# One order for early and middle expert rows: ScalarE casts their weights, VectorE gates middle rows in place, and their u tiles are asked for sooner

## The reference, cut to what matters

```python
q = xn @ wq                        # 8 heads x 2 halves x 128
top 16 of 128 keys for each half, then top 16 of their pair sums per head
gates = softmax(the 16 pair sums); expert = key_i * 128 + key_j
h = gelu(xn . peer_u[expert])      # 8 x 16 experts for each token
out = sum over those experts of gates * h * peer_v[expert]
```

## Time and profile before

| what | value |
|---|---|
| median of 3 runs | 3246.3 us (3240.91 to 3247.57) |
| the profiled execution's own time | 3233.7 us |
| span of its instructions | 3231.9 us |
| TensorE busy | 3097.7 us, 96% |
| VectorE busy | 2371.6 us, 73% |
| ScalarE busy | 1403.3 us, 43% |
| DMA over the span | 199 GB/s |
| mean granted TensorE clock | 0.977 |

### The profile page before, as it was taken

How to read it: one execution, slowest core, us unless ns; L and a number is a source line. 1 busy time by engine, 2 the same in 40 slices (tenths; PEclk the granted TensorE clock), 3 DMA queues, 4 the chain that set the end, 5 groups by cost and what they waited for, 6 DMA issues and landing times. The chain is left out here.

```text
span 3231.9 us, 52114 instructions
## 1 busy us (share of the span) xinstructions
PE 3097.7 (96%) x17744; PEld 2679.3 (83%) x17744; DVE 2371.6 (73%) x4997; ACT 1403.3 (43%) x2729; POOL 632.0 (20%) x556
## 2 busy tenths in 40 slices
PE   7899999999999999899999999999999998999999
PEld 5767776777867999888987799999789986899998
DVE  5667776776666677565978788788656887887887
ACT  5454333332336665475356333333465274333332
POOL 0000000000000000064434132222356061222221
PEclk9999999999999999899999999999999999999999
DMA  6115533434322545433545799999434518899996
GB/s 222 43 59 183 176 144 113 154 124 158 110 71 87 174 156 168 148 121 115 170 130 210 274 354 356 328 356 356 159 101 140 183 50 318 313 353 339 343 357 249
DMA packets 176414, 643.50 MB, mean 199 GB/s; under 512 B 20352, under 2 KB 20736, under 8 KB 175360
## 3 DMA queue, kind: packets, MB, share of 16 engines
q1 hardware_dynamic: 138672, 504.62, 45.0%
q0 software_dynamic: 36864, 134.23, 11.3%
q10 hardware_dynamic: 720, 2.71, 0.2%
HBM read 640.44 MB, written 1.05 MB: 198 GB/s over the span
## 5 line engine op out<-in xcount | busy, mean ns | idle before, releaser
L338 ACT ACTIVATE split<-ring 128x512 fp32r<-128x512 f32 (+1 forms) x644 | 397.6, 624 | 699.4 <-PE ps L224 666.5
L224 PE MATMUL ps<-hT,split 128*128 128x512 f32 (+1 forms) x3504 | 631.1, 341 | 6.5 <-DVEq L322 3.4
L224 PEld LDWEIGHTS ps<-hT,split 128*128 128x128 f32 x3504 | 546.5, 191 | 91.3 <-DVE hT L593 9.7
L347 POOL TENSOR_TENSOR split<-ring,split 128x512 fp32r<-128x512 f32 x184 | 244.3, 1338 | 1528.3 <-ACT split L338 1523.7
L2718 PE MATMUL ps<-h2F,gates 128*128 128x192 f32 x3008 | 519.2, 326 | 0.0
L347 DVE TENSOR_TENSOR split<-ring,split 128x512 fp32r<-128x512 f32 (+1 forms) x460 | 307.2, 678 | 283.3 <-ACT split L338 282.4
L2718 PEld LDWEIGHTS ps<-h2F,gates 128*128 128x128 f32 x3008 | 498.4, 190 | 17.1
L2784 ACT ACTIVATE split<-ring 128x512 fp32r<-128x512 f32 x504 | 317.4, 632 | 358.3 <-PE ps L2735 333.6
L2844 DVE TENSOR_TENSOR split<-ring,split 128x512 fp32r<-128x512 f32 x504 | 340.1, 689 | 118.0 <-ACT split L2784 115.4
L2708 POOL DMA_INDIRECT gates<-peer_rows,row_at x256 | 267.7, 1046 | 809.9 <-DVE row_act L2851 462.9
L2731 PE MATMUL ps<-split,chunk 128*128 128x512 f32 x512 | 232.1, 453 | 16.9 <-DVE chunk L2815 16.3
(11 more groups left out here) (394 smaller groups left out, 4758.2 us busy)
## 6 DMA issues: line engine op xcount, KB each, us to landing
ring<-peer_v SPq DMA_DIRECT2D x256, 512.0 KB
gates<-peer_u SPq DMA_DIRECT2D x200, 512.0 KB, 6.9
ring<-w_up SPq DMA_DIRECT2D x88, 512.0 KB, 3.8
ring<-w_choose SPq DMA_DIRECT2D x88, 512.0 KB, 3.5
ring<-w_mixing SPq DMA_DIRECT2D x68, 512.0 KB, 3.6
ring<-w_merge SPq DMA_DIRECT2D x64, 512.0 KB, 4.1
ring<-w_down SPq DMA_DIRECT2D x44, 512.0 KB, 3.7
mix_row_ring<-w_mod SPq DMA_DIRECT2D x40, 512.0 KB, 3.7
```

What stands on the lines that cost most here:

```text
L224: ins = nc.tensor.matmul(out, lhsT(a), rhs(b), start=first and n == 0, stop=last and n == len(PASSES) - 1)
L338: self.nc.scalar.activation(self.split[:, self.half_slot(s), 0, cols], self.ring[:, self.slot(s), cols], ACT.Copy).then_inc(self.high_read ...
L347: (ops or self.nc.vector).tensor_tensor(self.split[:, self.half_slot(s), 1, cols], self.ring[:, self.slot(s), cols], self.split[:, self.ha ...
```

## The change

In `experts_stage` the 34 early and middle rows now form one uniform list in `order`. Their weights are cast by ScalarE between the two halves of `high(j)`, and VectorE makes their lows between the two halves of `low(j)`. The middle rows are gated in place by VectorE at steps 1, 5, 9, 13, 17 and 21. `weigh` is left for late rows. In `choose_stage` the six middle u tiles are asked for among the last w_choose tiles. In `first_block` one sum of the modulation goes from place 5 to place 9.

```diff
-            up_sums = [(2, merge_rows[3]), (5, out_rows[0]), *(...)]
+            up_sums = [(2, merge_rows[3]), (9, out_rows[0]), *(...)]
 choose_stage, SyncE:
             for t in range(RAW, n_tiles):
                 slot_free(t - RAW)
                 weights.fetch(sp, t // RAW, t % RAW)
+                if 0 <= t - HC - RAW < MID:
+                    q = t - HC - RAW
+                    sp.dma_start(k.row_ring[:, q, :], tile(k.peer_u, l * (NK - EARLY) + q)).then_inc(k.mid_in, 16)
             for s in range(SPLIT):
                 slot_free(n_tiles - RAW + s)
                 ahead.fetch(sp, 0, s)
             ahead.begun = SPLIT
-            for q in range(MID):
-                sp.dma_start(k.row_ring[:, q, :], tile(k.peer_u, l * (NK - EARLY) + q)).then_inc(k.mid_in, 16)
 experts_stage:
-    order = [*((True, j) for j in range(EARLY)), (False, 0), (False, 1),
-             *(x for r in range(rows - 2) for x in ((True, EARLY + r), (False, r + 2))), (True, NK - 2), (True, NK - 1)]
+    given = EARLY + MID
+    order = [*((True, j) for j in range(given - 2)),
+             *(x for q in range(MID, rows) for x in ((True, EARLY + q - 2), (False, q))), (True, NK - 2), (True, NK - 1)]
+    given_of = lambda j: one(k.early, j) if j < EARLY else k.mid[(j - EARLY) // 2][:, (j - EARLY) % 2, :]
-    places = sorted([*range(3, EARLY, 4), *(t for t in range(EARLY + 2 * MID, len(order)) if is_v[t]), *range(EARLY + 2 * MID + 1, len(order) - 8, 6)])
+    places = sorted([*range(3, given, 4), *(t for t in range(given, len(order)) if is_v[t]), *range(given + 3, len(order) - 8, 6)])
 ScalarE:
+            def given_high(j):
+                if j >= EARLY:
+                    act.wait_ge(mid_gated, j - EARLY + 1)
+                act.wait_ge(halves_used, (j + SPLIT) * 2 - 2)
+                nc.scalar.activation(k.weight[:, j % 2, 0:DENSE], given_of(j), ACT.Copy).then_inc(weight_step, 1)
             def high(j):
                 act.wait_ge(weights.loaded[j % RAW], 16 * (j // RAW + 1))
                 for half, cols in enumerate(weights.halves):
+                    if half and j < given:
+                        given_high(j)
...
+            for j in range(SPLIT):
+                given_high(j)
...
-                if not v and n >= MID:
+                if not v:
                     activate(n)
 VectorE:
-            def split_early(j):
-                w, high = one(k.early, j), k.weight[:, j % 2, 0:DENSE]
-                dve.wait_ge(halves_used, (j + SPLIT) * 2 - 2)
-                nc.vector.tensor_copy(high, w).then_inc(weight_step, 1)
+            def split_given(j):
                 dve.wait_ge(weight_step, j + 1)
-                lows(w, j % 2)
+                lows(given_of(j), j % 2)
+            def gate_mid(q):
+                nc.vector.tensor_tensor(given_of(EARLY + q), given_of(EARLY + q), dense[:, :, q], ALU.mult).then_inc(mid_gated, 1)
             def weigh(q):
...
-                if q >= MID:
-                    dve.wait_ge(gelu_done, q - MID + 3)
+                dve.wait_ge(gelu_done, q - MID + 3)
...
             def low(j):
                 for half, cols in enumerate(weights.halves):
+                    if half and j < given:
+                        split_given(j)
...
-                if t + SPLIT < EARLY:
-                    split_early(t + SPLIT)
                 if not v:
                     weigh(n)
+                if t % RAW == 1 and t // RAW < MID:
+                    gate_mid(t // RAW)
```

More of the change, by code:

```diff
@@ L1567, in first_block @@
             up_places = [4 + 3 * t // 2 for t in range(3 * DC)]
-            up_sums = [(2, merge_rows[3]), (5, out_rows[0]), *((up_places[(n + 1) * DC - 1] + 2, p) for n, p in enumerate(up_rows))]
+            up_sums = [(2, merge_rows[3]), (9, out_rows[0]), *((up_places[(n + 1) * DC - 1] + 2, p) for n, p in enumerate(up_rows))]
             ffn_up_stage(k, w_up, tokens, w_down, ffn_norm, ModRows(k, up_rows, up_places, up_sums) if first else None)
@@ L2660, in experts_stage @@
     rows_there = lambda n: 16 * (l * len(range(n % ROW_SLOTS, 2 * sums, ROW_SLOTS)) + n // ROW_SLOTS + 1)
-    with stage(nc, *WEIGHT_SEMS, "u_in_0", "u_in_1", "u_in_2", "u_in_3", "u_done", "gelu_done", "weight_step", "weighted", "kept_0", "kept_1", "turned", "added", "stored", "ahead_high", "ahead_low",
+    with stage(nc, *WEIGHT_SEMS, "u_in_0", "u_in_1", "u_in_2", "u_in_3", "u_done", "gelu_done", "mid_gated", "weight_step", "weighted", "kept_0", "kept_1", "turned", "added", "stored", "ahead_high", "ahead_low",
                "row_step", "row_gelu", "row_weighed", *Norm.SUMS, weights=weights) as (
-            block, high_ready, low_ready, halves_used, u_in_0, u_in_1, u_in_2, u_in_3, u_done, gelu_done, weight_step, weighted, kept_0, kept_1, turned, added, stored, ahead_high, ahead_low,
+            block, high_ready, low_ready, halves_used, u_in_0, u_in_1, u_in_2, u_in_3, u_done, gelu_done, mid_gated, weight_step, weighted, kept_0, kept_1, turned, added, stored, ahead_high, ahead_low,
             row_step, row_gelu, row_weighed, squared, sums_done):
@@ L2816, in lows @@
                 ins.then_inc(weighted, 1)
-            def split_early(j):
-                w, high = one(k.early, j), k.weight[:, j % 2, 0:DENSE]
-                dve.wait_ge(halves_used, (j + SPLIT) * 2 - 2)
-                nc.vector.tensor_copy(high, w).then_inc(weight_step, 1)
+            def split_given(j):
                 dve.wait_ge(weight_step, j + 1)
-                lows(w, j % 2)
+                lows(given_of(j), j % 2)
+            def gate_mid(q):
+                nc.vector.tensor_tensor(given_of(EARLY + q), given_of(EARLY + q), dense[:, :, q], ALU.mult).then_inc(mid_gated, 1)
             def weigh(q):
                 j, buf = q + EARLY, q % 2
-                high, active = k.weight[:, buf, 0:DENSE], k.mid[q // 2][:, q % 2, :] if q < MID else k.gelu[:, buf, 0:DENSE]
-                if q >= MID:
-                    dve.wait_ge(gelu_done, q - MID + 3)
+                high = k.weight[:, buf, 0:DENSE]
+                dve.wait_ge(gelu_done, q - MID + 3)
                 dve.wait_ge(weighted, j + 2)
                 dve.wait_ge(halves_used, v_used(j - 2))
-                nc.vector.tensor_tensor(k.gated[:, 0:DENSE], active, dense[:, :, q], ALU.mult).then_inc(weight_step, 1)
-                dve.wait_ge(weight_step, j * 2 - EARLY + 1)
+                nc.vector.tensor_tensor(k.gated[:, 0:DENSE], k.gelu[:, buf, 0:DENSE], dense[:, :, q], ALU.mult).then_inc(weight_step, 1)
+                dve.wait_ge(weight_step, j * 2 - given + 1)
                 nc.vector.tensor_copy(high, k.gated[:, 0:DENSE]).then_inc(weight_step, 1)
-                dve.wait_ge(weight_step, j * 2 - EARLY + 2)
+                dve.wait_ge(weight_step, j * 2 - given + 2)
                 lows(k.gated, buf)
@@ L2866, in _ @@
             for j in range(SPLIT):
-                split_early(j)
+                split_given(j)
             for t, (v, n) in enumerate(order):
```

## The result

The changed kernel takes 3217.1 us (median of 10 runs, 3208.7 to 3238.8) against 3255.0 us of the kernel before (median of 10 runs, 3240.9 to 3262.7): a ratio of 0.9908, with a 95% interval of 0.9883 to 0.9932. That is 0.92% or some 30 us less by the ratio (22 to 38 us by its interval), and 28.7 us less was forecast; the two medians lie further apart, 37.9 us. The ten times of the changed kernel fall in two groups, seven from 3208.7 to 3222.6 us and three from 3234.5 to 3238.8 us, so a median depends on which group has more of them.

What follows compares the result with a forecast made beforehand. TensorE, busy 96%, bounds the kernel; only its waits and low clock before the late rows can be won. 2 x (3.4 + 6.65 + 1.3 - 0.6 - 0.1) = 21.3, plus 0.9 and 6.5: 28.7 off 3246.3 gives 3217.6 us, range 3208 to 3232.

Steps and rivals of the forecast that it cites:

- Middle rows: Combines 27 to 32: without gating, cast and lows right ahead of TensorE, no gap or half clock; 6.65 us less per layer.
- Combines 10 to 27: Early expert rows: moving the cast off VectorE gives it room, so combines run at 2.34 us; 3.4 us less per layer.
- The cast on ScalarE: 128x192 weight copy between both halves of `high`: 0.36 us, hidden; 0.1 us more per layer at the stage's start.
- The start: Combines 0 to 10, DMA bound: 1.3 us of 3.7 won per layer, less 0.6 for sooner gathers and 0.1 for the cast.
- Rival B: DMA sets the whole early part, gathers holding back v tiles beyond tile 10; early part wins nothing, 3225.8 us; chance 0.10.
- The u tiles: Scatter start: asking sooner for the middle u tiles makes layer 1 like layer 2; 0.9 us less.
- Place 9: Up stage: sum moved from place 5 avoids the bias-step wait and lost clock; 6.8 less 0.3 for later copy, 6.5 us less.
- Rival A: Early part still set by VectorE or ScalarE's hand-over; combines 10 to 27 keep 43.2 us, 3224.4 us; chance 0.11.
- Rival C: Middle stall moves to the first late rows, whose weights come late; 13.3 us lost, 3230.9 us; chance 0.05.
- D: Late rows start from full DMA queues and take 5.12 us each; 37.6 us more, 3255 us; chance 0.04.
- Rival E: Something unseen hides a stall, the change does little: within 6.5 us of the old time; chance 0.04.
- The signs: Expected in the profile: combines 2.34 us apart from 10 to 32, no gap above 0.3; wrong if ScalarE awaits v tiles after tile 10.

Runs made afterwards that it cites:

- run 4: Kernel before, early rows only: cast on ScalarE, weights between the halves; middle rows as before. Combines 27 to 32 take 18.10 and 18.34 us, 10 to 27 39.76 and 39.77.
- run 3: Changed kernel with the casts back on VectorE, same new order; in layer 2 combines 10 to 27 take 39.77 us and 27 to 32 11.67 us.
- run 1: Changed kernel without the sooner u tiles and with the sum back at place 5: 3229.1 us, ratio 0.9934 to the kernel before.
- run 9: The changed kernel unaltered, measured again in a second series on another chip: 3233.3 us, ratio 0.9916 to the kernel before.
- run 5: Kernel before with only the early weights' place moved between VectorE's two v tile lows, cast still on VectorE: combines 10 to 27 take 39.75 and 39.92 us.
- Run 6: Kernel before with only the early casts moved to ScalarE, weights' lows still after both v tile lows: combines 10 to 27 take 42.09 and 41.40 us.
- run 11: Changed kernel with only gathers 2 to 11 held back for the early rows in front: first ten combines 23.4 us, 32 combines 74.8 us, in both layers.
- Run 7: Kernel before with only the middle u tiles asked for sooner: VectorE's scatter start to combine 0 takes 69.3 us in layer 1, 67.9 in layer 2.

## Why the prediction was right, and where it was not

The saving was right: 28.7 us forecast, 27.9 us measured in the traces at the places aimed at (29.0 us without the scatter stretches), 29.9 us by the ratio (3255.0 x 0.0092). That the time itself came out at 3217.1 us for a forecast of 3217.6 us is luck: the base of 3246.3 us was 8.7 us under the median of ten runs, the medians then differed by 37.9 us, 9.2 us more than forecast, and the two cancel. The same kernel's second series had its median at 3233.3 us, just outside the range of 3208 to 3232 us. By its own terms:

- **Middle rows**, 6.65 us a layer: 7.15 and 6.68 us measured. The mechanism stands by run 4 (the stall stays without the new order) and run 3 (it goes with it, wherever the cast is done); which part of the new order does it stays open.
- **Combines 10 to 27**, 3.4 us a layer: 2.9 and 3.0 us measured, and 3.4 us in runs 1, 3, 4 and 9 (39.8 us). What is left in the profiled execution is the one combine that waits for its v tile. Here the size was about right and the step was wrong. "Four steps and a dot are 9.3 us of the 9.36 us that four combines take: no room for its waits" was the reason given, and the cast's way to ScalarE was to be the cure. Run 3 makes the cast on VectorE and loses nothing; run 5 moves only the weights' place in VectorE's queue and gains all. The step that failed is this sum: it was 0.6 us too large in four combines, and it missed that the last thing done in a step was the first thing wanted. Run 6 shows what moving the cast is worth by itself: 1.1 and 1.8 us of the 3.4.
- **The cast on ScalarE**, taken as 0.36 us and hidden: 0.36 us measured (mean of 64), and hidden. It is not needed for combines 10 to 32 (run 3).
- **The start**, 1.3 less 0.6 less 0.1 = 0.6 us a layer: 1.0 and 1.3 us measured. The 0.6 us taken off for the dot that asks sooner for the next gather was too much here, but the stretch itself varies: run 1 has 0.4 us less than before in layer 1 and 1.5 us in layer 2. That DMA keeps most of the 3.7 us held for this change: TensorE waits there for lows whose tiles landed late. It is no limit of the stage: with the gathers held back all of it can be had (run 11). The 411 GB/s "in its first 20 us" is a window of 6 us; over combines 0 to 10 it was 399 and 390 GB/s, at a share of 1.00.
- **Rival B** was right in its mechanism and wrong in its reach. In the row at the start of this stage the DMA engines move 402 GB/s at a share of 1.01, and with fewer gathers ahead the v tiles are in time (run 11). The rule of the Trainium skill (DMA: Bandwidth & Descriptors, Queues, rings and completion order), turns between the queues that have work, agrees with the even shares of the two queues there, 51.1% to 50.9% and 50.0% to 51.8%. But the gathers cost 2.1 and 2.4 us in combines 0 to 10 and 0.6 us in 10 to 27 (0.1 us in runs 1, 3 and 9), not the 3.4 us of the rival. That fits the 1.7 us of slack that the prediction gave a low in the steady part.
- **The u tiles**, 0.9 us: nothing. "With the tiles there early, layer 1 becomes like layer 2" failed: the row showed a wait of TensorE, and the step took the 0.9 us between two stretches for its price. Run 7 takes the wait away and leaves the stretch; what looked like a difference of layers is within the spread of a stretch of 67.9 to 69.8 us. The fetches ahead of it lose nothing in the changed kernel, as costed (from place 16 to the scatter it is 1.3 us longer, in a stretch of 1075 us, which takes 1071 to 1077 us over the fourteen traces).
- **Place 9**, 6.5 us: 6.9 us in the trace. The 0.3 us for the later copy was not needed.
- **Rival A** (the hand-over still paces): no. Combines run 2.34 us apart with two semaphores from ScalarE in each step. **Rival C** (the stall moves to the late rows) and **D** (late rows starved): no, 477.17 us and 477.24 us from combine 32 to the end, and in the 9.1 us behind combine 32 of layer 1 the DMA engines are at a share of 0.80 where it was 0.67. D's price took the window's 341 GB/s for a limit; it was what the rows moved while each took 4.92 us. **Rival E** (the change does little): no, by the interval of the ratio.
- **The signs.** Two of the signs named as wrong or unwanted did show, in a small measure. ScalarE waits for v tiles after tile 10, six times in layer 1 and five in layer 2 up to combine 32, and in layer 1 one gap is 0.4 us where none above 0.3 us was expected. Nearly all of these waits are covered. Combine 0 to 32 at "near 77.5 us" was hit (77.4 and 77.7 us), though the forecast's own terms give 78.0 us (88.65 - 10.65).

With the median of ten runs as its base and the same 28.7 us the forecast would have been 3226.3 us, still in the range.

## What to carry to other kernels

When an engine's step looks full, compare the order of its work with the order in which its results are wanted before moving work elsewhere: an in-order queue that makes the first thing wanted last is late with room to spare. A wait that the trace shows at the start of a stage is worth its length only if nothing else paces the stage; price it from several stretches of the same code, not from one pair. And where a stage starts at the limit of its DMA engines, hold back what isn't due: three gathers fewer in the 35 us about the start of layer 2's stage went with 2 to 3 us less in each layer's early rows, and the late rows were no longer for it. By the times of whole runs this gain is not settled.

## What was not expected of the hardware

The granted clock in the first 500 us changes from one execution to the next with the same code, and goes with most of the spread of the times. The changed kernel again (run 9) had these windows:

```profile
100.00:150.00 50.00, 44.43 (x251) 39.83 (x252) 21.60 (x54) 16.66 (x39) 0.00 (x0) 0.86 0.21 69
...
200.00:250.00 50.00, 46.65 (x182) 27.99 (x182) 21.50 (x61) 19.34 (x46) 0.00 (x0) 0.80 0.21 74
...
450.00:500.00 50.00, 47.65 (x204) 39.66 (x203) 30.93 (x54) 18.27 (x32) 0.00 (x0) 0.80 0.27 95
```

The first profile, over the last of these:

```profile
450.00:500.00 50.00, 47.64 (x225) 39.06 (x225) 37.09 (x72) 23.23 (x43) 0.00 (x0) 0.90 0.28 99
```

In its first 100 us run 9 has a clock of 0.86 where the first profile has 0.93. Its sum at place 2 starts at 517.45 us, 14.7 us later than the 502.74 us of the first profile of the same kernel, of 17.7 us between their spans. ScalarE's L1340 starts at 237.0 us in the first and 6.8 us later in run 9, its L1348 at 416.0 and still 6.8 us later, its L1427 at 497.3 and 14.7 us later. Over the fourteen traces the start of this sum, with the same code ahead of it in all, lies between 493.7 and 520.2 us; the stretch from combine 32 of layer 1 to layer 2's scatter is the next, 777.9 to 788.2 us. Over the ten runs of the result the mean granted clock goes from 0.968 (3238.8 us) to 0.979 (3208.7 us), some 2.9 us for each 0.001 by a line through all ten. Why the clock is granted so differently there was not tried. It means that one pair of executions can hide or double a gain of 15 us, and that here a change of 5 us is told from stretches of the trace at a granted clock of 1.00, or from many more runs than these.
